# A two-block transformer kernel: row tiles as row sums, half-head rotations by transfers inside SBUF, values ahead of exponentials, four stores

## What is computed

```python
def rope(x, pos):                      # first block, on q, k, qi, ki
    x1, x2 = xf[..., :half], xf[..., half:]
    return concatenate([x1 * cos - x2 * sin, x2 * cos + x1 * sin])

mod  = silu(c)     @ w_ada[layer] + b_ada[layer]      # 1024 -> 6144
modc = silu(c_ctx) @ w_ada[layer] + b_ada[layer]
sh1, sc1, g1, sh2, sc2, g2 = split(mod, 6)
u = (rmsnorm(x) * (1 + sc1) + sh1) @ w_in[layer]
x = x + g1 * (concat([gla, short_conv, neighbourhood_attention]) @ w_out[layer])
h =  rmsnorm(x) * (1 + sc2) + sh2
x = x + g2 * conv_ffn(h)               # 1024 -> 5632 -> 2816 -> 1024
```

## Time and profile before

| | us |
| --- | --- |
| median of 3 runs | 1489.95 (1489.83 to 1494.48) |
| the profiled execution | 1486.99 |
| its span, first to last instruction | 1485.2 |
| PE busy | 1402.2 (94%) |
| DVE busy | 987.8 (67%) |
| ACT busy | 710.4 (48%) |
| POOL busy | 47.4 (3%) |

### The profile page before, as it was taken

How to read it: one execution, slowest core, us unless ns; L and a number is a source line. 1 busy time by engine, 2 the same in 40 slices (tenths; PEclk the granted TensorE clock), 3 DMA queues, 4 the chain that set the end, 5 groups by cost and what they waited for, 6 DMA issues and landing times.

```text
span 1485.2 us, 22067 instructions
## 1 busy us (share of the span) xinstructions
PE 1402.2 (94%) x8641; PEld 1201.1 (81%) x8641; DVE 987.8 (67%) x1907; ACT 710.4 (48%) x1195; POOL 47.4 (3%) x66
## 2 busy tenths in 40 slices
PE   6999998998999999999999999999899988899997
PEld 4777897778977886577888888888788867899997
DVE  5597685977743385645798897665533655788854
ACT  5537565366534632633444444312344636566642
POOL 0000000000000012000000000000000210000000
PEclk9999999999999999998999999999899999999998
DMA  6633556334452221642345445567233331365552
GB/s 242 227 131 125 159 184 201 129 100 159 140 168 85 67 95 53 230 168 100 128 156 169 158 156 175 172 221 243 96 112 100 105 99 56 128 196 177 183 185 81
DMA packets 61752, 217.48 MB, mean 146 GB/s; under 512 B 6960, under 2 KB 9008, under 8 KB 61392
## 3 DMA queue, kind: packets, MB, share of 16 engines
q1 hardware_dynamic: 59152, 205.55, 42.1%
q0 software_dynamic: 2352, 10.52, 2.1%
q10 hardware_dynamic: 144, 0.00, 0.0%
HBM read 214.99 MB, written 1.05 MB: 145 GB/s over the span
## 4 chain that ended last, share of the span: by engine, by line
PE 80%; DVE 8%; ACT 7%; issue 3%; DMA 1%; DVEq 0%; ACTq 0%
PE bank L561 19%; PE bank L563 19%; PE bank L562 19%; PE bank L577 3%; ACT WHI L1299 2%; DVE WLO L1832 2%; PE bank L1137 1%; ACT L1299 1%; PE bank L622 1%; PE bank L623 1%; PE bank L624 1%; PE bank L531 1%; PE bank L736 1%; PE bank L599 1%; PE bank L1265 1%
## 5 line engine op out<-in xcount | busy, mean ns | idle before, releaser
L1832 DVE TENSOR_TENSOR WLO<-RAWB,WHI 128x1024 fp32r<-128x1024 f32 (+1 forms) x280 | 333.5, 1193 | 271.5 <-ACT WHI L1299 270.3
L561 PE MATMUL bank<-NHI,WHI 128*128 128x256 f32 (+1 forms) x1440 | 481.7, 335 | 15.8 <-DVE WLO L1832 8.6
L562 PE MATMUL bank<-NLO,WHI 128*128 128x256 f32 (+1 forms) x1440 | 474.0, 329 | 0.0
L563 PE MATMUL bank<-NHI,WLO 128*128 128x256 f32 (+1 forms) x1440 | 474.0, 329 | 0.0
L1299 ACT ACTIVATE WHI<-RAWB 128x1024 fp32r<-128x1024 f32 (+1 forms) x280 | 287.5, 1029 | 194.7 <-PE bank L563 131.5
L561 PEld LDWEIGHTS bank<-NHI,WHI 128*128 128x128 f32 x1440 | 275.7, 191 | 51.9 <-issue 14.7
L562 PEld LDWEIGHTS bank<-NLO,WHI 128*128 128x128 f32 x1440 | 275.9, 192 | 25.5 <-issue 2.2
L563 PEld LDWEIGHTS bank<-NHI,WLO 128*128 128x128 f32 x1440 | 275.5, 191 | 24.2
L1299 ACT ACTIVATE CF<-bank,PRM 128x512 f32<-128x512 f32 (+1 forms) x88 | 59.1, 671 | 178.7 <-PE bank L563 175.9
L561 PE MATMUL bank<-HHI,WHI 128*128 128x512 f32 (+1 forms) x352 | 119.3, 339 | 0.0
L563 PE MATMUL bank<-HHI,WLO 128*128 128x512 f32 (+1 forms) x352 | 119.2, 339 | 0.0
(11 more groups left out here) (319 smaller groups left out, 1928.4 us busy)
## 6 DMA issues: line engine op xcount, KB each, us to landing
RAWB<-in_ws SPq DMA_DIRECT2D x364, 512.0 KB, 3.4
RAWB<-in_ws SPq DMA_DIRECT2D x32, 384.0 KB, 3.5
NB<-in_nab POOLq DMA_DIRECT2D x12, 256.0 KB, 3.7
K<-in_c POOLq DMA_DIRECT2D x2, 896.0 KB, 4.7
K<-in_c POOLq DMA_DIRECT2D x1, 1344.0 KB, 7.9
X<-in_xt SPq DMA_DIRECT2D x4, 256.0 KB, 5.8
X<-in_xt POOLq DMA_DIRECT2D x1, 1024.0 KB, 6.5
CREP<-in_crep POOLq DMA_DIRECT2D x1, 1024.0 KB, 5.0
```

Of the source, the lines that this page charges most:

```text
L561: nc.tensor.matmul(o, hi[:, w], xh, start=(i == 0), stop=False)
L562: nc.tensor.matmul(o, hi[:, w], xl, start=False, stop=False)
L563: ins = nc.tensor.matmul(o, lo[:, w], xh, start=False, stop=(i == slabs - 1))
L1832: V.tensor_tensor(WLO[:, k % SPL, 0:w], RAWB[:, u % RAW, 0:w], WHI[:, k % SPL, 0:w].bitcast(F32), ALU.subtract).then_inc(S("lo_ready"), 1)
```

## The change

- Modulation tiles 5 to 10 (the sixth to the eleventh) become dots: `DOT_TILES` is now 5 to 23. The first 20 units (`DOTS_FIRST`, tiles 5 to 9) are summed on DVE beside layer 0's first twelve projection units, one or two units each (`DOTS_PROJ`), from an own replicated vector `CREP1`, loaded and passed through silu at the start of the stage, and with an own product buffer `DP1`; both share memory with `EQ`, `QX` and `EQ0`, so POOL and DVE wait for those dots before these are written. The feed-forward part keeps 26 units in its upper half and gets 30 instead of 26 in its lower half. All of tiles 5 to 10's `rows`, `columns`, `copy_rows` and `modulation` go.
- The rotation of five of six groups is made by POOL's transfers: two or four for a group, each moving 32 partitions of `Z` to the other half-head's place in `RT2`; DVE multiplies from `RT2`. The sign moves from `perm` into the sine table. The last group keeps PE's product. `rope(0)` moves from t = 2 to 3, `rope(1)` from 4 to 5, the index from 5 to 6, `rope(2)` and `rope(3)` from 10 and 12 to 11 and 13, `rope(4)` from 14 to beside the attention's second item. `divide(l, 2)` stands ahead of the split of its tile.
- The two `kb` tiles are made by `native`; the first group of rows stands at t = 2 instead of 1.
- In the second block's projections `values(1)` stands ahead of `Exp`, and `Ln` comes behind tile 4's copy; ACT splits one unit more ahead there and ahead of `cross_exponentials`.
- `modulate` makes its vector ahead of `stats`, and DVE and ACT step by halves of 256 columns.
- The output is stored in four pieces of two slabs.

```diff
-NATIVE_FROM = Z1["pin"]
+NATIVE_FROM = Z1["kb"]
-ROTATE_AT = {1: 0, 3: 1, 9: 2, 11: 3, 13: 4, 15: 5}
-INDEX_AT = 5
-ROWS1 = (1, 4, 7, 10)
+ROTATE_AT = 15
+INDEX_AT = 6
+ROWS1 = (2, 4, 7, 10)
...
-BESIDE_ROWS = 5
-DOT_TILES = range(11, 24)
+DOT_TILES = range(5, 24)
+DOTS_FIRST = 20
+DOTS_PROJ = (1, 1, 1, 2, 2, 1, 2, 2, 2, 2, 2, 2)
-DOTS_DOWN = (4, 4, 4, 4, 4, 4, 2, 0)
+DOTS_DOWN = (5, 5, 5, 5, 4, 4, 2, 0)
...
-            sp.wait_ge(S("x_new"), KS * (DEPTH + 2))
-            sp.dma_start(out, X[:, :, 0:T]).then_inc(S("stored"), 16)
-            sp.wait_ge(S("stored"), 16)
+            for k in range(0, KS, 2):
+                sp.wait_ge(S("x_new"), KS * (DEPTH + 1) + k + 2)
+                sp.dma_start(out[:, k:k + 2, :], X[:, k:k + 2, 0:T]).then_inc(S("stored"), 16)
+            sp.wait_ge(S("stored"), 16 * KS // 2)
...
+                for g, (name, k) in enumerate(ROPES1[:-1]):
+                    z = Z1[name]
+                    pool.wait_ge(S("z_freed"), NZ1 * l + z + k)
+                    if l > 0 or g > 0:
+                        pool.wait_ge(S("rope_freed"), len(ROPES1) * l + g)
+                    for h in range(2 * k):
+                        pool.dma_start(RT2[32 * h:32 * h + 32, 0:k, :], Z[32 * (h ^ 1):32 * (h ^ 1) + 32, z:z + k, :]).then_inc(S("rot_moved"), 16)
...
+                if l == 0:
+                    pool.dma_start(CREP1[:], crep).then_inc(S("ld_crep"), 16)
                 pool.dma_start(K2[:], c2).then_inc(S("ld_c2"), 16)
...
+                if l == 0:
+                    pool.wait_ge(S("dot_summed"), DOTTED[DOTS_FIRST])
                 nc.gpsimd.memset(QX[:, 512:1024], 0.0).then_inc(S("pads_set"), 1)
...
-                    h = i - 3
-                    if uc and 0 <= h < 2 * BESIDE_ROWS:
-                        rows(3, 4 * (h % 2), 4 * (h % 2) + 4, h // 2, BESIDE_ROWS)
...
-                    if uc and m == 1:
-                        columns(3, BESIDE_ROWS)
                     stats_behind(m, n, SQ2)
-                if uc:
-                    rows(5)
                 spread_scales("r_tok", "r_spread", n // P)
-                held[4] = (S("t_ready"), me.nth("t_ready", KS))
+                held[4] = (S("t_ready"), me.nth("t_ready", KS * seqs))
                 fm_side_by_side(AHEAD, n, rhs, "up_freed", "x_split")
-                if uc:
-                    columns(5)
...
                 rest()
+                values(1)
+                split_to(me.u + 1 + AHEAD)
                 act.wait_ge(S("act_chain"), me.nth("act_chain", 4))
                 A(GTA, GTA, ACT.Exp, scale=-1.0).then_inc(S("act_chain"), 1)
-                act.wait_ge(S("act_chain"), me.nth("act_chain"))
-                A(GTA, GTA, ACT.Ln, bias=1.0).then_inc(S("gln_ready"), 1)
-                values(1)
                 for i in range(NFIRST, NZ2):
                     tile(i)
+                    if i == NFIRST:
+                        split_to(me.u + 1 + AHEAD)
+                        act.wait_ge(S("act_chain"), me.nth("act_chain"))
+                        A(GTA, GTA, ACT.Ln, bias=1.0).then_inc(S("gln_ready"), 1)
...
                     if i == 8:
+                        split_to(me.u + 1 + AHEAD)
                         cross_exponentials()
...
+                    if g < len(ROPES1) - 1:
+                        dve.wait_ge(S("rot_moved"), MOVED[-1] * l + MOVED[g])
+                        turned = RT2[r, 0:k, :]
+                    else:
+                        dve.wait_ge(S("rot_ready"), me.nth("rot_ready"))
+                        turned = bank[5][:].rearrange("p (a t) -> p a t", a=k)
+                    V.tensor_tensor(rt, turned, bc(c1v("sin")[r, :], k), ALU.mult).then_inc(S("rope_freed"), 1)
...
+                def dots_beside(j):
+                    for _ in range(DOTS_PROJ[j] if l == 0 and j < len(DOTS_PROJ) else 0):
+                        dot()
+
                 for i in range(NFIRST):
                     rest()
+                    dots_beside(i)
                 for u in range(4):
                     rest()
+                    dots_beside(NFIRST + u)
...
                 for i in range(NFIRST, NZ2):
                     rest()
+                    dots_beside(4 + i)
                     if i == 5:
                         dve.wait_ge(S("gln_ready"), me.nth("gln_ready"))
```

More of the change, by code:

```diff
@@ L49 @@
 NZ1 = len(TILES1)
-NATIVE_FROM = Z1["pin"]
+NATIVE_FROM = Z1["kb"]
 ATTEND_FROM = 14
 ROPES1 = (("kiwi", 1), ("qi", 2), ("qa", 2), ("ka", 2), ("qb", 2), ("kb", 2))
-ROTATE_AT = {1: 0, 3: 1, 9: 2, 11: 3, 13: 4, 15: 5}
-INDEX_AT = 5
-ROWS1 = (1, 4, 7, 10)
+ROTATE_AT = 15
+INDEX_AT = 6
+MOVED = [16 * 2 * sum(k for _, k in ROPES1[:g + 1]) for g in range(len(ROPES1) - 1)]
+ROWS1 = (2, 4, 7, 10)
 ROW_GROUP_AT = 12
@@ L145, in stream @@
             add([UNIT])
+            dots(DOTS_PROJ[i] if l == 0 else 0)
             rows(2 if l == 0 and i in ROWS2 else 0)
-        add([2 * VW] * 4 + [UNIT] * (NZ2 - NFIRST))
-        rows(BESIDE_ROWS * ROW_U if l == 0 else 0)
+        for j, width in enumerate([2 * VW] * 4 + [UNIT] * (NZ2 - NFIRST)):
+            add([width])
+            dots(DOTS_PROJ[NFIRST + j] if l == 0 and NFIRST + j < len(DOTS_PROJ) else 0)
         add([UNIT] * KS)
-        rows(ROW_U if l == 0 else 0)
         for m in range(2 * FT):
@@ L168 @@
 DOT_N = [2 if t < ROW_TILES + 4 else 1 for t in DOT_TILES for _ in range(4)]
+DOTTED = [sum(DOT_N[:k]) for k in range(len(D_AT) + 1)]
 SPLIT_W = [w for w in range(NW) if not NATIVE[w]]
@@ L230, in build @@
         RT = sb(st, "RT", [P, 512])
+        RT2 = sb(st, "RT2", [P, 2, T])
         WI = sb(st, "WI", [P, TT, IDXH])
@@ L277, in build @@
         BK = sb(st, "BK", [P, 3072])
+        end = ExitStack()
+        CREP1 = sb(end, "CREP1", [P, 2, D])
+        DP1 = sb(end, "DP1", [P, D])
+        end.close()
         EQ = sb(st, "EQ", [P, 3, TC])
@@ L425, in _ @@
                     if w == DOT:
-                        sp.wait_ge(S("dot_summed"), sum(DOT_N[:D_AT.index(u - RAW) + 1]))
+                        sp.wait_ge(S("dot_summed"), DOTTED[D_AT.index(u - RAW) + 1])
                     elif w == ROW:
@@ L1711, in _ @@
                     values(0)
+                    act.wait_ge(S("ld_crep"), 16)
+                    A(CREP1[:], CREP1[:], ACT.Silu).then_inc(S("crep_ready"), 1)
                 else:
@@ L2084, in attend @@
                         if k == 1:
+                            rope(4, "qk_roped")
                             rope(5, "qk_roped")
@@ L2102, in _ @@
                         gated(OB, range(4), 4, 4)
+                    if t == 2:
+                        divide(l, 2)
                     rest()
@@ L2251, in modulate, with residual @@
                         rest()
-                    for c in range(n // T):
-                        w = slice(c * T, (c + 1) * T)
-                        if s < KS:
-                            ins = V.scalar_tensor_tensor(TB2[:, s, w], X[:, s, w], GM[:, s, c:c + 1], bank[4][:, w], ALU.mult, ALU.mult)
                     if s < KS:
-                        ins.then_inc(S("t_ready"), 1)
+                        scaled(s, 0)
                     if s >= 1:
-                        dve.wait_ge(S("xh_ready"), me.nth("xh_ready"))
-                        dve.wait_ge(S("t_ready"), me.nth("t_ready"))
-                        for c in range(n // T):
-                            w = slice(c * T, (c + 1) * T)
-                            ins = V.scalar_tensor_tensor(NLO[:, s - 1, w], TB2[:, s - 1, w], MOD[:, l, shift + s - 1, c:c + 1],
-                                                         NHI[:, s - 1, w].bitcast(F32), ALU.add, ALU.subtract)
+                        for c in range(seqs):
+                            ins = low(s - 1, c)
                         ins.then_inc(S("x_split"), 1)
-            def residual(l, n, gate, units, sq, dots=(), beside=None):
+                    if s < KS and seqs == 2:
+                        scaled(s, 1)
+            def residual(l, n, gate, units, sq, dots=()):
                 for m in range(KS):
@@ L2272, in residual @@
                         dot()
-                    if m == 2 and beside is not None:
-                        beside()
                     add_squares(m, n, sq)
@@ L2541, in _ @@
                 me.from_bank_0()
-                residual(l, n, G1, 1, SQ2, beside=(lambda: modulation(3, BESIDE_ROWS)) if uc else None)
+                residual(l, n, G1, 1, SQ2)
                 dve.wait_ge(S("wo_freed"), me.nth("wo_freed", KS))
-                stats(n)
                 modulate(l, n, f"nffn{l}", SH2, SC2)
                 for p in range(FT + 2):
-                    if uc and p == 2:
-                        modulation(5)
                     if p < FT:
```

76 lines of the change are left out of this document (40 added, 36 removed).

## The result

The changed kernel takes 1476.66 us (median of 10 runs) against 1489.2 us for the kernel before, measured again in the same runs: a ratio of 0.9921, 95% interval 0.9900 to 0.9941. So it is faster, as forecast, but by some 12 us, where 25 were forecast. Its profiled execution took 1476.74 us, 10.25 less than that of before.

The account below looks back on a forecast made before the run. PE was taken to bound the kernel, 80% of the chain. Terms -10.5 + 1 - 3 - 3.9 - 6.8 + 0 - 1.5 = -24.7 gave 1462.3 profiled, 1465 median; range 1452 to 1474, upward to 1481.

Parts of the forecast that it names:

- Part 1: First block: moved rotations, native `kb` and moved rows take 4.5 us off layer 0 and 6 off layer 1, -10.5.
- the ring: Layer 0's projection, second block: two-dot tiles need 250 GB/s; 303 were carried elsewhere, landings up to 5.2 us keep up.
- The sign named for all this: First block, layer 0: the first attention item comes some 4.5 us earlier than 93.25.
- rival B: First block: rotation transfers land late, at 9.5 us costing 12 us a layer (1489), at 10.5 slower (1497); chance 0.07.
- Part 2: Second block, layer 0's projection: PE gains 5 us early, idles for DVE ahead of `sums`; +1 us, bounds -4 to +8.
- rival A: Second block, layer 0's projection: the ring or DVE holds it; +10 (1475), up to 1483; chance 0.15.
- Part 3: Layer 0's attention, second block: ten calls of rows go, 12.2 us, mostly becoming idle time; -3, bounds 0 and -9.6.
- Part 4: Behind layer 0's attention: `rows(5)` and two `columns` go, `modulate` by halves; -3.9, bounds -2 and -5.
- The term for tile 10's rows: Behind layer 0's attention: `rows(5)`, 3.40 us, filled a wait lasting 1.73 us without rows; -1.7.
- Part 5: Second block, layer 1: values' wait, half-speed stretch, a quarter of the `WLO` wait, `modulate`; -6.8, bounds -3 and -9.
- Part 6: Feed-forward: 0, +5 if DVE's cover is gone; end, four stores: -1.5, bounds 0 and -2.5.
- Rival C: Layer 0's attention and `sums`: PE's new idle time brings six more half-speed stretches, +10 (1475); chance 0.1.

Follow-up runs that it names:

- e2: The first block's changes alone, on the kernel before: 1490.16 us, ratio 1.0019.
- e5: Kernel before with the second block's small changes only (values first, earlier splits, halves in `modulate`, four stores), no new dots: 1470.63 us, ratio 0.9897.
- e6: Kernel before with ACT's order alone changed: values ahead of `Exp` and `Ln`, one unit split earlier: 1476.2 us, ratio 0.9929.
- e9: e5 plus the two `kb` tiles in native form, rotations still on PE: 1465.25 us, ratio 0.9849.
- e11: e5 with one store of 1 MB at the end instead of four: 1475.2 us, ratio 0.9906.
- e1: Changed kernel without the new dots, modulation tiles 5 to 10 as rows again: 1470.58 us, ratio 0.988.
- e8: e1 with the two `kb` tiles split again: 1476.64 us, ratio 0.993.
- e10: e5 plus rotations by transfers in their later places, `kb` split, first rows at tile 1: 1474.85 us, ratio 0.9905.
- e3: Changed kernel with the first group of rows back at tile 1: 1477.08 us, ratio 0.9918.
- e7: e1 with first rows at tile 1 and `rope(1)` ahead of layer 1's sums over `PL`: 1472.21 us, ratio 0.99.
- e4: Changed kernel with rope and gates moved ahead of dots on DVE in layer 0's projection: 1472.89 us, ratio 0.9897.
- e12: e9 with tiles 5 to 10 as dots, placed on DVE behind the rope and the gates: 1466.09 us, ratio 0.9856.

## Why the direction was right and the size was not

**Part 1, the first block: forecast -10.5, measured nothing (e2, e5).** Three steps of it failed.

The first is the stall of 3.5 us in layer 1, taken from one execution as if it were always there. The kernels e5, e6 and e9 have the same instructions there, and it is 1.7, 1.9 and 1.8 us in them (e11: 1.9). In the kernel before, ACT had waited 4.0 us for one late unit ahead of it.

The second is that a removed wait was counted as gained without asking what PE meets next. It meets the first index score, at tile 6, which needs `rope(1)`. The change had moved that rope behind the split of tile 5, and in layer 1 behind two sums. DVE in the changed kernel, layer 1 (start, duration):

```profile
241.62 1.23 DVE L1845 TENSOR_TENSOR WLO<-RAWB,WHI 128x1024 fp32r<-128x1024 f32 x1 [3.70 <-ACT WHI L1311]
242.76 1.94 DVE L2130 TENSOR_TENSOR PL<-PL 128x1024 f32<-128x1024 f32 x2
244.73 0.69 DVE L2026 TENSOR_TENSOR RT<-RT,K 128x512 f32<-128x512 f32 x1
245.34 0.68 DVE L2027 TENSOR_TENSOR Z<-Z,K 128x512 f32<-128x512 f32 x1
246.13 0.69 DVE L2030 TENSOR_TENSOR Z<-Z,RT 128x512 f32<-128x512 f32 x1
```

PE was ready at 245.1 and began at 246.9, and ran at half speed for the next tile. In layer 0 the first rows, moved out of an idle hole, cost their 1.06 us as forecast; beyond it the second group, two tiles behind the first, waited 1.9 us for the ring, and its records took 2.1 us in place of 1.06. The ring was weighed for the second block's dots and not here. A half-speed stretch behind the 3.6 us for the head weights was counted at a half (0.7) and came whole (1.5). At the attention, `rope(4)` and `rope(5)` together let the second item wait 1.2 to 1.5 us, against 0.5 forecast. The sign named for all this, layer 0's first attention item 4.5 us earlier than 93.25, came at 91.09, 2.2 earlier.

The third is the sign of the transfers' share. Of the 10.5 us the native tiles made 3.8 (per layer 2.4 on DVE less 0.5 on PE), and they measured 5 to 7: e5 to e9 is 5 us by medians and 7 by ratios, e1 to e8 6 and 7. The other 6.7, the rotations with what they moved, came out as a loss of about 5 (e9 to e1; with split `kb`, e5 to e10, it lies within the noise). So the native tiles are all of the first block's gain, and the rest eats it. Why the transfers lose is shown only as far as the waits go, above; the trace has no single line of 5 us.

One part of it was a term of the sum: the landing of a group was priced as that of one transfer, 4.7 us. One transfer of 64 KB took 3.3 us in the median over the run and 4.0 between 24 and 110, 6.8 at most, and its issue 0.50 us of POOL. But DVE needs the last of the four that `rope(1)` takes, and in the changed kernel that one landed 8.3 us (layer 0) and 6.7 us (layer 1) behind the first one's issue; over all kernels with transfers it was 6.0 to 9.1. DVE waited for none in the changed kernel, with 1.3 us to spare in layer 0, where `rope(1)` stands one tile later than before. In three of the other seven it did wait: 1.9 us in e3, 1.3 twice in e7, 0.6 in e10. So the transfers allow no earlier `rope(1)`, and rival B's 9.5 us was near for this group, its waits of 12 us a layer were not. By the rule cited for B from the Trainium skill (SBUF — State Buffer, "SBUF: two separate sides"), DVE can lock GpSimd out of the port that it writes a transfer's descriptors through; whether that held these transfers up no run here tells, since the issue took 0.50 to 0.53 us in every kernel and the ring's traffic ran beside. The estimate of 2.15 us worked out from the Trainium skill (DMA: Bandwidth & Descriptors, "Anatomy of one DMA — SWDGE (gpsimd) path") lies under the measured 3.3, and the row's 4.7 over it.

**Part 2, the second block's projection: forecast +1, measured +5.7.** The sum for DVE was right: `sums` was put near 486 and began at 488.2, behind unbroken work of DVE from 441.6 on. In the chain in order of time:

```profile
483.69 1.28 DVE DP L1938
484.99 0.02 issue
485.02 1.28 DVE DP L1938
486.31 0.06 DVE GQ L2512
486.37 0.33 issue
486.70 1.49 DVE GQ L2512 x3
488.18 0.04 issue
488.23 6.71 PE bank L1101 x32
```

The half-speed stretch is in that last row: 6.71 us against 4.77 in the earlier trace rows, 1.9 where I had 1.7. So the gates cost 4.8 us, under the 6.7 of the sum. The step that failed is that the work queued on DVE was asked for one waiting reader only. The rope ahead of the gate projection stands behind dots as well: it began at 456.52 right behind one, PE waited 2.2 us and ran the next unit at half speed, 1.4 us more, 4.6 in all with the products around the wait. Both readers are cured by order alone (e4). A second term was put at nothing, the ring. The two groups of row tiles that stay in this projection share it with the dots, and their records took 1.6 us longer (two lines before, then after):

```profile
424.71 1.07 PE L531 MATMUL bank<-RAWB,CV 128*32 128x512 f32 x8
436.81 1.06 PE L531 MATMUL bank<-RAWB,CV 128*32 128x512 f32 x8
...
422.94 1.78 PE L552 MATMUL bank<-RAWB,CV 128*32 128x512 f32 x8
435.77 1.95 PE L552 MATMUL bank<-RAWB,CV 128*32 128x512 f32 x8
```

Units landed in 4.3 us in the median there, against 3.3 before. This part of the loss stays in e4 (1.9 us), and with 1.8 us that DVE waited for dot units it is what is seen of rival A. The three terms, 4.8, 4.6 and 1.6, are the 11.0 us between the 5.3 won by the values and the 5.7 lost.

**Part 3, layer 0's attention: forecast -3, measured -1.5** in the changed kernel, the same in e3 and -1.4 in e4. The mechanism was right, most of the 12.2 us of rows turned into idle time. The size can't be told better than to 2 us: nine other kernels that keep the rows there took 0.3 to 2.6 us longer than before for the same stretch. PE's waits at 598:640, before and after:

```profile
PE bank L736 <- DVE ZB L2453: 0.3, 1, 0.3
...
PE bank L757 <- ACT PT L1311: 7.9, 5, 2.0
PE bank L1226 <- DVE GS L1867: 1.6, 1, 1.6
```

**Part 4, behind it: forecast -3.9, measured -2.8.** The term for tile 10's rows was mis-sized. The 3.40 us of the earlier trace rows were in part a half-speed stretch. At full speed, in e1 (second line) and e9, the same 16 records take 1.92 us, hardly more than the 1.74 that PE idles without them; in the other eight traces with rows they take 3.36 to 3.64. And the idle time without them puts the next records at half speed (third line, the changed kernel, against 1.16 in e1):

```profile
686.14 3.48 PE L531 MATMUL bank<-RAWB,CV 128*32 128x512 f32 x16
...
682.90 1.92 PE L542 MATMUL bank<-RAWB,CV 128*32 128x512 f32 x16
...
689.45 2.08 PE L806 MATMUL bank<-CST,GR 128*128 128x128 f32 x8 [1.74 <-DVE GR L1867]
```

The granted clock says the same, in the changed kernel at 688:690 (the last but two figure):

```profile
688.00:690.00 2.00, 0.55 (x2) 0.55 (x3) 0.97 (x6) 0.20 (x1) 0.00 (x0) 0.50 0.00 0
```

From the start of the norm's sums to the feed-forward part it takes 11.4 us before. With the halves of `modulate` and the rows kept it takes 8.9 us in e1 and e9, 10.5 to 10.6 in e5, e7, e8 and e10 and 12.1 in e11; with the halves and no rows 10.4 in the changed kernel and 9.8 to 10.4 in e3, e4 and e12. So rows kept in that hole are about free (10.3 against 10.2 in the mean), and taking them out wins nothing clear of chance. The halves of `modulate` were worth 0.9 there (3.20 to 2.32 ahead of the first product), near the 0.6 forecast.

**Part 5, layer 1: forecast -6.8, measured -6.8,** but of other terms: 3.4 for the values (3.7 and a half-speed stretch of 1.5, less a new wait of 1.7 for the gates ahead of `sums`), 1.4 for the later wait for `WLO` (3.6 to 2.0), and 1.9 behind these, of which 1.4 in the attention are luck. A wait of 2.52 us stands there in both traces; before, PE ran at half speed behind it, and in the changed kernel not.

**Part 6: forecast 0 and -1.5, measured 0 and -2.2.** Layer 0's feed-forward part takes the same time to 0.01 us, with eight more sums on DVE (120 - 72 in all, 40 of them in the projection). The last store was priced by the shortest landing of a load, 3.4; 3.0 lie between the last scaling and the end.

**The range** reached from 1452 to 1481 and held the time; the direction was right. The size was not: of the 14.4 us missing between the two profiled executions, 8.3 are part 1, 4.7 part 2, 1.5 and 1.1 parts 3 and 4, and the last store gave 0.7 back; 0.5 came back between the parts. Rival C's 1475 is nearer than the forecast, but not by its mechanism: it wanted six more half-speed stretches, and there were 13 before and 13 after, 74 us in both, with a mean granted clock of 0.976 in both. The waits moved, and the stretches moved with them.

## What to carry to other kernels

A wait that a profile shows is worth what stands behind it: before it is counted as gained, go on along the waiting engine to the next thing it needs from the same producer, and look whether the edit has moved that later. When work is put on an engine with slack, list every reader of that engine's results in the stretch, and put the work behind them; order took the dots' cost from 6 us to less than the runs can tell (e12 against e9). When one operation waits for several transfers, price the last one's landing from the first one's issue. A long row may be a half-speed stretch, and a stall may be one late transfer: compare it with the same instructions elsewhere before it becomes a term of a sum.

## What the runs showed of the hardware

Half-speed stretches fall by chance as well as by cause. The same wait of 2.52 us was followed by one in one kernel and by none in another, and code that is identical (103 to 212) differed by up to 2.5 us between traces. One costs about 1.4 to 1.9 us. So filling a hole of PE with work that could stand elsewhere can be free (16 records of rows: 8.9 to 12.1 us with them, 9.8 to 10.4 without).

Transfers of 64 KB from SBUF to SBUF on POOL's queue took 3.3 us in the median and up to 6.8 beside a busy ring, 0.50 us of POOL each. Four of them, issued one behind the other for `rope(1)`, took 6.0 to 9.1 us from the first issue to the last landing. The ring's units took 4.0 us beside them over the first block, against 3.7 before.

A store's tail is short: 3.0 us behind the last result with 256 KB, 5.2 with 1 MB.
